# Two-layer diffusion backbone with a top-2 mixture of experts: experts worked in groups of 32 rows

## The reference: what is computed

```python
def route(h_flat, w_router, b_router):
    s = jax.nn.sigmoid((h_flat @ w_router).astype(jnp.float32))
    ...                      # best group of 4 experts, then its top 2 of 16
    return jnp.sum(jax.nn.one_hot(idx, N_EXPERTS) * w[..., None], axis=1)

a = jnp.einsum('td,edf->tef', xc, w1_l)      # 1024 -> 512
b = jnp.einsum('td,edf->tef', xc, w3_l)      # 1024 -> 512
u = jax.nn.silu(a) * b * gc[..., None]
return jnp.einsum('tef,efd->td', u, w2_l)    # 512 -> 1024
```

```
layer 0: 40 37 15 44 96 75 56 69 113 77 96 136 52 29 29 60
layer 1: 45 80 16 49 11 10 5 16 13 96 56 45 25 2 10 33
```

## Time and profile before

| | us |
|---|---|
| median of 3 runs (1323.61 to 1328.58) | 1327.61 |
| span of the profiled execution | 1325.8 |
| experts of layer 0, first up product to end of last down product | 428.7 to 733.8 |
| experts of layer 1, the same | 1031.5 to 1296.4 |
| PE busy in the span | 1081.6 |

### The profile page before, as it was taken

How to read it: one execution, slowest core, us unless ns; L and a number is a source line. 1 busy time by engine, 2 the same in 40 slices (tenths; PEclk the granted TensorE clock), 3 DMA queues, 4 the chain that set the end, 5 groups by cost and what they waited for, 6 DMA issues and landing times.

```text
span 1325.8 us, 18500 instructions
## 1 busy us (share of the span) xinstructions
PE 1081.6 (82%) x6246; PEld 604.7 (46%) x6247; DVE 345.4 (26%) x812; ACT 208.4 (16%) x487; POOL 79.0 (6%) x126
## 2 busy tenths in 40 slices
PE   2799989988981999999899189989892898788771
PEld 1446447765450544444346044647642454344430
DVE  2201147565342100101011430157624011000002
ACT  1110023432010111111101211023300111011001
POOL 2000000001002000000000300000101000000001
PEclk8899999989985999999999689999985799999896
DMA  9923116576135899999369671313645699999993
GB/s 330 374 91 127 64 70 238 202 258 226 43 131 208 319 396 395 398 397 384 122 227 397 214 269 64 127 64 128 240 158 198 234 332 397 396 396 397 397 397 110
DMA packets 142294, 328.60 MB, mean 248 GB/s; under 512 B 6552, under 2 KB 8760, under 8 KB 142240
## 3 DMA queue, kind: packets, MB, share of 16 engines
q1 hardware_dynamic: 125424, 287.84, 58.9%
q0 software_dynamic: 7856, 25.61, 5.4%
q10 hardware_dynamic: 8960, 14.40, 3.1%
HBM read 308.10 MB, written 19.73 MB: 247 GB/s over the span
## 4 chain that ended last, share of the span: by engine, by line
PE 56%; DMA 29%; DVE 7%; ACT 3%; issue 3%; POOL 2%; SPq 0%; ACTq 0%; DVEq 0%; POOLq 0%
DMA ring<-in_w 23%; PE S L1217 17%; PE S L1398 10%; PE S L1327 6%; PE O L1281 4%; PE T L1155 3%; PE AUX L1172 3%; DMA ring<-in_w_ada 3%; PE S L1432 2%; PE T L1432 2%; PE S L1248 2%; PE S L1402 2%; ACT R L643 1%; PE S L1437 1%; DVE R L916 1%
## 5 line engine op out<-in xcount | busy, mean ns | idle before, releaser
L1217 PE MATMUL S<-ring,hT 128*128 128x512 f32 (+1 forms) x576 | 226.0, 548 | 2.3 <-ACT hT L587 2.3
L1402 PE MATMUL S<-ring,R 128*64 128x256 f32 x1472 | 181.1, 405 | 33.0 <-DMA ring<-in_w 28.3
L1402 PEld LDWEIGHTS S<-ring,R 128*64 128x64 f32 x1472 | 114.5, 146 | 106.3 <-DMA ring<-in_w 40.3
L1217 PEld LDWEIGHTS S<-ring,hT 128*128 128x128 f32 x576 | 108.0, 191 | 104.3 <-issue 98.6
L1398 PE MATMUL S<-ring,R 128*128 128x512 f32 x320 | 144.1, 610 | 6.5 <-issue 3.3
L1155 PE MATMUL T<-cst,R 128*128 128x128 f32 (+1 forms) x497 | 80.1, 292 | 64.2 <-DVE R L793 30.4
L1088 DVE SCALAR_TENSOR_TENSOR R<-R,S 128x256 f32<-128x256 f32 (+1 forms) x33 | 16.6, 502 | 412.7 <-ACT R L694 412.7
L1155 PEld LDWEIGHTS T<-cst,R 128*128 128x128 f32 (+1 forms) x497 | 60.2, 151 | 93.4 <-DVE R L793 30.7
L1398 PEld LDWEIGHTS S<-ring,R 128*128 128x128 f32 x320 | 62.1, 195 | 87.2 <-issue 82.4
L1437 PE MATMUL S<-ring,R 128*64 128x512 f32 x368 | 84.0, 598 | 9.6 <-DMA ring<-in_w 5.7
L1327 PE MATMUL S<-ring,hT 128*128 128x512 f32 x192 | 85.6, 607 | 2.3 <-issue 2.3
(11 more groups left out here) (143 smaller groups left out, 756.8 us busy)
## 6 DMA issues: line engine op xcount, KB each, us to landing
ring<-in_w SPq DMA_DIRECT2D x96, 2048.0 KB, 11.5
ring<-in_w_ada SPq DMA_DIRECT2D x24, 2048.0 KB, 8.1
ring<-in_w_in SPq DMA_DIRECT2D x8, 2048.0 KB, 10.8
R<-x_d POOLq DMA_DIRECT2D x45, 256.0 KB, 5.7
ring<-in_w_out SPq DMA_DIRECT2D x4, 2048.0 KB, 9.8
R<-mod_d SPq DMA_DIRECT2D x12, 512.0 KB, 9.6
y_d<-R ACTq DMA_DIRECT2D x46, 128.0 KB, 5.3
y_d<-R ACTq DMA_DIRECT2D x20, 256.0 KB, 6.5
```

Source lines behind the costliest of these rows:

```text
L1217: ins = pe.matmul(S[:, i % 4, 0:width], hT[:, k, t * P:(t + 1) * P], w[:, k, :], start=(k == 0), stop=(k == KC - 1))
L1402: ins = pe.matmul(S[64 * h:64 * h + 64, i, 0:256], xT[:, half, k % 4, k // 4, 0:64], part[i][:, k, h * 256:h * 256 + 256], start=(k == 0), ...
```

## The change

Experts are worked in groups of 32 rows. Every expert starts at a multiple of 32 rows in `x_d` and `y_d`, so both buffers are zeroed beforehand by POOL, 30 DMAs of 512 KB, issued once the first projection is done. The array is used as four 32-column tiles. The down product of a group is issued in the item of the next group, after that one's up products. The loads of all experts are now part of the fixed list: w1 and w3 of expert e+2 wait for `w13_free` (after the first up product of expert e+1), its w2 for `w2_free` (after the first down product in expert e+1's first item). Behind them, in order, come the gate row `gF` and three projection weights of layer 1. One buffer each holds the fetched rows (`xg`), the transposed rows (`xT`) and the result (`y_s`).

```diff
-TILE = 64
-MAXW = TOK // P
+ROWS = 32
+MAXG = TOK // ROWS
+SETS = 2
...
+            last[slot] = (s["w2_free" if part == 2 else "w13_free", l], e + 1)
...
+                    pool.wait_ge(s["zeros_made"], 1)
+                    pool.wait_ge(s["proj_done"], 1)
                     for m in range(DEPTH):
+                        for b in range(x_tiles[m]):
+                            pool.dma_start(x_d[m][b * P:(b + 1) * P, :], zeros).then_inc(s["tail_zeroed"], 16)
...
+                fetch(0)
+                with pool.Fori(0, n) as i:
                     pool.wait_ge(s["counts_ready"], l + 1)
+                    pool.wait_ge(s["rows_flipped", l], r_flips)
+                    fetch(i + 1)
+                    pool.reg_add(r_flips, r_flips, 1)
...
+                with act.Fori(2, n) as i:
...
+                    act.wait_ge(s["up1_done", l], r_next)
+                    gate_up()
...
+                    act.wait_ge(s["up3_done", l], r_next)
+                    take_rows()
...
+                    act.wait_ge(s["down_done", l], r_done)
+                    act.wait_ge(s["y_stored", l], r_stored)
+                    copy(y_s, y_bank).then_inc(s["y_out", l], 1)
+                    act.wait_ge(s["y_out", l], r_next)
+                    store(i - 1)         # four DMAs of 32 KB
...
+                grp, start = R[12][:, 0:NE], R[13][:, 0:NE + 1]
+                ch.step(dve.tensor_scalar(grp, cnt, (ROWS - 1) / 2, 1.0 / ROWS, ALU.add, ALU.mult))
+                ch.step(dve.tensor_scalar(grp, grp, 2.0 ** 23, None, ALU.add))
+                ch.step(dve.tensor_scalar(grp, grp, -2.0 ** 23, 1.0, ALU.add, ALU.max))
...
+                def up(bank, w, up_done):
+                    for k in range(KC):
+                        for q in range(4):
+                            ins = pe.matmul(bank[32 * q:32 * q + 32, :], xT[:, k // 2, k % 2, :], w[:, k, P * q:P * q + P],
+                                            start=(k == 0), stop=(k == KC - 1))
+                    ins.then_inc(s[up_done, l], 1)
...
+                def down(w, first=False):
+                    for q in range(4):
+                        for j in range(4):
+                            ins = pe.matmul(y_bank[32 * j:32 * j + 32, :], uT[:, 32 * q:32 * q + 32], w[:, q, 256 * j:256 * j + 256],
+                                            start=(q == 0), stop=(q == 3))
...
+                def item(e, first, rep):
...
+                    if first:
+                        pe.wait_ge(*full[0])
+                    pe.wait_ge(s["rows_taken", l], r_next)
+                    pe.wait_ge(s["t2_done", l], r_done)
+                    up(a_bank, own[0], "up1_done")
+                    pe.wait_ge(s["rows_in", l], r_have)
+                    flip_rows(first)
+                    pe.wait_ge(s["u_done", l], r_done)
+                    flip_up()
+                    if first:
+                        pe.wait_ge(*full[1])
+                    up(b_bank, own[1], "up3_done")
+                    pe.wait_ge(s["u_taken", l], r_done)
+                    pe.wait_ge(s["y_out", l], r_done)
+                    down(prev[2], first)
...
+                def others(e, at, rep):
+                    pe.wait_ge(slot_full[3 * (e % SETS) + 2], 16 * rep + where["e", l, e, 2][1])
+                    n = pe.value_load(ngroup[0:1, l, at], min_val=1, max_val=MAXG)
+                    pe.reg_mov(r_more, n)
+                    with pe.If_ne(r_more, 1), pe.Fori(1, n):
+                        item(e, False, 0)
```

More of the change, by code:

```diff
@@ L309, in build @@
             load_expert(0, 1, part)
-        loads.append("experts0")
-        for i in range(6):
-            count[i] += 16 * (NE // 2 - 1)
+        for e in range(2, NE):
+            for part in range(3):
+                load_expert(0, e, part)
+        loads.append("gf0")
+        for u, slot in zip(UNITS[:3], (0, 1, 2)):
+            load_in(1, u, slot)
+        loads.append("drain0")
+        for i in (3, 4, 5):
             last[i] = None
-        for u, slot in zip(UNITS, (0, 1, 2, 3, 4)):
+        for u, slot in zip(UNITS[3:], (3, 4)):
             load_in(1, u, slot)
@@ L325, in build @@
             load_expert(1, 1, part)
-        loads.append("experts1")
+        for e in range(2, NE):
+            for part in range(3):
+                load_expert(1, e, part)
+        loads.append("gf1")
         def slot_view(slot, k):
@@ L420, in store_mod @@
                     pool.dma_start(dst, modrow[32 * q:32 * q + 2, l * N_ADA + n0:l * N_ADA + n1, :]).then_inc(s[stored], 16)
[L422 to L427 removed]
+            r_flips, r_stored = (pool.alloc_register(f"pool_{n}") for n in ("flips", "stored"))
             n_ssq = 0
@@ L562, in square_sum @@
                 squares[0] += 1
-                act.activation(junk, X[:, t, :], ACT.Square, accum_out=ssq[:, c0 + c:c0 + c + 1]).then_inc(s["act_ssq"], 1)
-            n_items, n_more = act.alloc_register("act_items"), act.alloc_register("act_more")
-            act.reg_mov(n_items, 0)
-            act.reg_mov(n_more, 0)
-            tiles = act.alloc_register("act_tiles")
-            wide, narrow, next_first, before, down = (act.alloc_register(f"act_{n}")
-                                                      for n in ("wide", "own_wide", "next_first", "before", "down"))
+                act.activation(out, X[:, t, :], ACT.Square, accum_out=ssq[:, c0 + c:c0 + c + 1]).then_inc(s["act_ssq"], 1)
+            r_done, r_next, r_stored = (act.alloc_register(f"act_{n}") for n in ("done", "next", "stored"))
             for l in range(DEPTH):
@@ new lines, in take_rows, with gate_up, store @@
+                def take_rows():
+                    copy(xT, x_bank.rearrange("p (j t h) -> p h j t", j=2, h=4)).then_inc(s["rows_taken", l], 1)
+                def gate_up():
+                    act.activation(th, a_bank, ACT.Tanh, scale=0.5).then_inc(s["tanh_done", l], 1)
+                def store(item):
+                    for j in range(4):
+                        act.dma_start(y_d[l][ds(ROWS * item, ROWS), 256 * j:256 * j + 256],
+                                      y_s[32 * j:32 * j + 32, :]).then_inc(s["y_stored", l], 16)
@@ L743, in _ @@
+                act.wait_ge(s["counts_ready"], l + 1)
+                act.wait_ge(s["down_done", l], r_done)
+                act.wait_ge(s["y_stored", l], r_stored)
+                copy(y_s, y_bank).then_inc(s["y_out", l], 1)
+                act.wait_ge(s["y_out", l], r_next)
+                store(n - 1)
                 act.wait_ge(s["counts_ready"], l + 1)
@@ L783, in _ @@
                 ada_out(x)
-            n_items = dve.alloc_register("dve_items")
-            dve.reg_mov(n_items, 0)
-            wide = dve.alloc_register("dve_wide")
+            r_done, r_next = (dve.alloc_register(f"dve_{n}") for n in ("done", "next"))
             for l in range(DEPTH):
@@ L1177, in _ @@
                 ada(x)
-            n_items = pe.alloc_register("pe_items")
-            pe.reg_mov(n_items, 0)
-            n_more, have, emptied, last_y = (pe.alloc_register(f"pe_{n}") for n in ("more", "have", "emptied", "last_y"))
-            pe.reg_mov(n_more, 0)
-            tiles = pe.alloc_register("pe_tiles")
-            wide, own_wide, now = (pe.alloc_register(f"pe_{n}") for n in ("wide", "own_wide", "now"))
+            r_done, r_next, r_have, r_more = (pe.alloc_register(f"pe_{n}") for n in ("done", "next", "have", "more"))
             for l in range(DEPTH):
@@ L1193, in _ @@
                 for k in range(KC):
-                    transposes(("hT", l, k), [xn[:, t, k * P:(k + 1) * P] for t in range(TT)])
+                    transposes(("hT", l, k), [xns[l][:, t, k * P:(k + 1) * P] for t in range(TT)])
                 taken(("hT", l, KC - 2))
@@ new lines, in _ @@
+                others(0, slice(0, 1), 0)
+                reps = (NE - 1) // SETS
+                with pe.Fori(0, reps) as rep:
+                    for e in range(1, SETS + 1):
+                        item(e, True, rep)
+                        others(e, ds(SETS * rep + e, 1), rep)
+                for e in range(1 + SETS * reps, NE):
+                    item(e, True, 0)
+                    others(e, slice(e, e + 1), 0)
+                pe.wait_ge(s["counts_ready"], l + 1)
+                pe.wait_ge(s["u_done", l], r_done)
```

465 lines of the change are left out of this document (163 added, 302 removed).

## The result

The changed kernel takes 1350.25 us (median of 4 runs, 1347.77 to 1352.41) against 1325.61 of the kernel before beside it: ratio 1.019, 95% interval 1.0165 to 1.0215. **Slower by 1.9%**, where 1324 was forecast. The profiled spans are 1350.7 and 1325.8.

What follows compares the result with a forecast made beforehand. Layer 0 was taken as bound by TensorE, layer 1 by weight loads. 1325.8 - 4.1 + 1.8 - 3.0 + 1.8 = 1322.3 us profiled, 1.8 under the median, so 1324; likeliest 1318 to 1333, eight in ten 1305 to 1358.

Steps and rivals of the forecast that it cites:

- What bounds the kernel now: Expert stages of the kernel before: layer 0 (305.1 us) bound by TensorE, layer 1 (264.9 us) by weight loads.
- The array: TensorE's work on a 32-row group: three blocks at 1.93 us plus transposes, together 6.6 us.
- Rival 3: TensorE: 32 weight columns or PE's own sequencer cost more; at 8.5 us a group 1386 us; chance 0.09.
- The two round trips: Single-buffer result-store and row-fetch loops: 4.4 to 7.5 and 4.2 to 6.9 us, taken as just under the group period.
- P = 6.6: Period of a group in the expert stages, taken as 6.6 us; 6.6 at best, 7.5 at worst.
- Rival 1: Store or fetch round trip sets the group period: 1352 us at period 7.5, 1341 at 7.2; chance 0.24.
- the recursion: Expert start times from group periods and weight landings; stages of 301.0 us in layer 0, 266.7 in layer 1.
- The loads: Expert weights reloaded later, some 2.2 us after the next expert starts; layer 0 gains 4.1 us, layer 1 loses 1.8.
- Edges: Before each layer's first product -1.5 us, bounds for both 0 and -3.5; behind the last product +0.9 a layer.
- The cold start: First group of a stage, at the lower clock in part: 2.5 us added, so the second starts at 9.0.
- Zeroing: 30 DMAs of 512 KB early on, done before the first value product: cost 0, some 70 us to spare.
- Projection weights ahead: Early loads of layer 1's projection weights: 0; gate row and these loads beside the gathers: between 0 and +2 us.

Runs made afterwards that it cites:

- light weights: From each layer's third expert only the first 128-row block of each weight matrix is loaded; stages: kernel before 301.6 and 217.7 us, changed kernel 242.6 and 165.6.
- both loops cut: Changed kernel with two result buffers and two fetch buffers: 1334.8 us, ratio 1.0062.
- the one-column matmul: Kernel with both buffers doubled and the w2 wait moved, w1 and w3 slots freed by a one-column matmul after the expert's last group: 1317.9 us, ratio 0.9935.
- one store of 128 lines: Changed kernel, each group's result stored by one 128 KB transfer to 128 consecutive 1 KB lines instead of four 32 KB stores: 1342.9 us, ratio 1.0134.

## Why the prediction was wrong, step by step

- **What bounds the kernel now: right.** With light weights layer 0 of the kernel before takes 301.6 of its 305.0 us, so it was bound by TensorE; layer 1 falls from 264.9 to 217.7, so it was bound by loads. (The slices were read a little wrong: number 19 moves 384 GB/s, and number 22 is full too.)
- **The array: right in the blocks, 0.7 us too much in the sum.** 1.95 and 1.91 against 1.93 taken; 5.86 a group against 6.6, as transposes and block heads overlap. Rival 3 falls. So does the 2.2 for a block that the prediction scaled from three column tiles in the Trainium skill, TensorE: Matmul & The Clock Gate, section Measured speedup vs the span model: 6.95 on one tile over 1.95 is 3.6 times.
- **The two round trips: this step failed.** It said "I take **P = 6.6**, with both loops just under it". The store loop was 7.2 in the median and 7.3 in the groups shown, so it and not TensorE's work set the group. The term that was mis-sized is the landing of 32 KB beside full engines: "some 4.4", from an assumed 1.2 us for each 128 KB. From the last issue to the copy it took 4.9; the page has 4.7 in the median, and the longest landing is 6.6. The step from 128 KB to 32 KB is worth 0.6 us, not 0.9. The other 0.2 to 0.3 are the pause before the first issue and slightly slower issues. The upper end of my own bounds, 7.5 with "if size doesn't help", held it. I had both loops within 0.1 us of the period and called that a forecast; a loop that varies from 6.0 to 8.5 can't be hidden by 0.1. The period taken was also more than the 5.86 that TensorE needs, so even loops of 6.6 would have set it.
- **Rival 1 is what happened.** Its price for P = 7.5, 1352, stands beside 1350.3; layer 0 has 320.9 where it gave 323.5, layer 1 274.3 where it gave 272.5. But the experiments show that it got there partly for another reason: doubling both buffers brings back 15.4 us (1350.3 to 1334.8), not the 28 that lie between P = 6.6 and 7.5. So the agreement of the total is luck in part, better than the mechanism. Nor is the price itself firm: worked again from its rules as they are written, the recursion gives 296.6 and 265.5 us at P = 6.6 and 321.6 and 271.0 at 7.5, up to 4.4 us from the recorded figures.
- **The loads: right in kind, short in size; the second step that failed.** The recursion gave layer 1 +1.8; it was +9.4, and nearly all of it is here: 274.3, 273.9 with both loops cut. "w1 is there after 5.3 and 2 of landing" is too short: with two loads issued together the first was there after 9.0 to 9.5 us at most gaps and 10.6 at the one shown, so 1.7 to 3.3 later than taken. The late freeing and the wait for w2 were both named (17.8 against 7 us, 9.2 against 3.7), but their price in layer 0 was lost in the recursion's total. Over both layers the wait is worth 9.8 us (7.9 alone), the freeing 7.1 by the one-column matmul and 5.5 more as before. Both signs that the prediction named for being wrong came: groups more than 7 us apart, and layer 1 longer than 270.
- **Edges.** The start of layer 0 is 4.1 us earlier; 1.5 was taken, bound 3.5. The cold start cost one block at 3.56 instead of 1.95; the second group came 6.6 after the first, not 9.0. Behind, +1.8 against 0.9; the single result buffer holds the last copy too (3.20 us in layer 1).
- **Zeroing: right.** No wait at the first value products, which come at 190.0 us, 2.2 earlier than before.
- **Projection weights ahead, gathers and hand-over: not as taken.** The stretch between the stages is 1.9 us longer, but that is a sum of two things. From the last down product to the first transposes of `hT` it takes 36.7 us against 32.0 before, 4.8 more, where 0.9 for the stores and at most 2 for the gathers were taken. The rest, up to layer 1's first up product, is 2.9 us shorter, where 1.5 was taken. The second result buffer brings back 1.4 of the 4.8; what the rest is no run shows.
- **What would have told it blind.** The landing row of 128 KB, 5.3 us, was the nearest row to a store of 32 KB, and I left it for a slope between two rows of different load.

## What to carry to other kernels

A change that makes one engine faster gives little while a loop of small transfers with a single buffer is longer than the engine's new time: count the loop with the landing time that such transfers have beside the bulk traffic, and double the buffer before tuning the engine. When two resources are near balance, look at what each wait really needs: a wait placed too early and slots freed too late cost 9.8 and 12.6 us here, more than the 18 us or so that 111 us of saved work brought in the end. Before judging a change by its total, run both kernels with the heavy traffic taken out; it shows what was saved and what was lost after.

## What the runs showed of the hardware

- A store of 32 KB lands in 2.5 us with light weights and in 4.7 beside the full ones (322 to 349 GB/s in the stages), a fetch of 128 KB in 2.4 and 5.3. Traffic doubles it; four times the bytes in a store add 0.6 to 0.8 (5.3 in the kernel before, 5.5 with one store of 128 lines).
- The same 128 KB store takes 9.5 us or 6.1 in the median from issue to release by its pattern alone (outer dimension 4 or 128), 70 us over the kernel.
- Two loads of 2 MB issued together after a gap are there after 9.0 to 10.6 and 14 to 15.4 us; in a running stream one lands every 5.5.
- Four 32-column tiles side by side work off the same number of moving columns 3.6 times as fast as one tile of 128 (1.95 against 6.95 us, the latter scaled from the earlier trace rows); each column meets a quarter of the weight columns.
- In layer 1 of the changed kernel the granted clock is 0.85 of full speed where the kernel of before had 0.94: TensorE stands for 7.5 us before an expert, then does its first up block at the lower of its two levels (granted 0.50), 3.64 us instead of 1.95. While the loads set the pace this costs nothing: the block is done before w3 lands, some 5.5 us behind w1. With light weights, where these waits are gone, the clock is 0.99.
- The doubled result buffer's code on ScalarE, with its branches by parity, costs 0.3 to 0.5 us of a group; TensorE's branches by parity cost nothing that the period shows (5.83 to 5.94 with them).
